# A fused two-block kernel: another order for the recurrence that runs between block products

## The reference, cut to what matters

```python
proj = h @ w_in[l]                       # g_q, g_f, g_i, g_z are 8 heads x 128 columns each
q = silu(q_raw); logf = log(lb + (1 - lb) * sigmoid(fr)); k = (1 - lb) * sigmoid(-fr)
def step(S, xs):
    qn, kn, vn, ln = xs
    b = cumsum(ln, axis=2)
    b_last = b[:, :, -1]
    inter = einsum('bhcd,bhde->bhce', qn * exp(b), S)
    diff = b[:, :, :, None, :] - b[:, :, None, :, :]
    decay = exp(where(tril, diff, -inf))
    A = einsum('bhtd,bhtsd,bhsd->bhts', qn, decay, kn)
    intra = einsum('bhts,bhse->bhte', A, vn)
    k_dec = kn * exp(b_last[:, :, None, :] - b)
    S_new = exp(b_last)[..., None] * S + einsum('bhsd,bhse->bhde', k_dec, vn)
    return S_new, inter + intra
```

## Time and profile before

| | |
|---|---|
| three runs, median (lowest to highest) | 1989.35 us (1988.53 to 1993.09) |
| profiled execution: its own time | 1990.67 us |
| profiled execution: span of the trace | 1988.9 us |
| PE, DVE, ACT, POOL busy | 94%, 74%, 47%, 15% |
| seven steps of pairs, 1258.02 to 1756.38 us | 498.36 us |
| in them PE, DVE, ACT busy | 383.80, 308.88, 238.16 us |

### The profile page before, as it was taken

How to read it: one execution, slowest core, us unless ns; L and a number is a source line. 1 busy time by engine, 2 the same in 40 slices (tenths; PEclk the granted TensorE clock), 3 DMA queues, 4 the chain that set the end, 5 groups by cost and what they waited for, 6 DMA issues and landing times.

```text
span 1988.9 us, 30107 instructions
## 1 busy us (share of the span) xinstructions
PE 1860.4 (94%) x11014; PEld 1649.0 (83%) x11014; DVE 1470.0 (74%) x2190; ACT 926.6 (47%) x1406; POOL 289.9 (15%) x283
## 2 busy tenths in 40 slices
PE   9999999999999999999999999868778777789999
PEld 8888888888888878878899999867777776778999
DVE  6666688888888876688787877756566566558986
ACT  6543433333333633245565666635445435446433
POOL 3500000000000024420011111031132122111021
PEclk9999999999999999999999999979978888899999
DMA  6244244444444356744477777444453444462452
GB/s 266 106 171 168 82 167 172 171 169 169 169 170 174 121 202 231 248 166 137 117 201 193 184 198 193 117 102 101 106 118 95 105 114 107 108 210 85 139 179 86
DMA packets 80505, 304.07 MB, mean 153 GB/s; under 512 B 8584, under 2 KB 14216, under 8 KB 67728
## 3 DMA queue, kind: packets, MB, share of 16 engines
q1 hardware_dynamic: 66640, 256.49, 37.3%
q0 software_dynamic: 13312, 43.00, 12.2%
q10 hardware_dynamic: 448, 3.17, 0.4%
HBM read 288.44 MB, written 14.18 MB: 152 GB/s over the span
## 4 chain that ended last, share of the span: by engine, by line
PE 75%; DVE 11%; ACT 7%; issue 6%; DMA 1%; POOL 0%; DVEq 0%; POOLq 0%; ACTq 0%; SPq 0%; another core or an unknown queue 0%
PE ps_p L918 13%; PE ps_p L920 13%; PE ps_p L919 13%; PE ps_p L1322 4%; PE ps_p L1321 4%; PE ps_p L1323 4%; ACT w_hi L1917 2%; DVE w_lo L2917 1%; PE ps_o L1083 1%; PE ps_t L1571 1%; PE ps_t L1572 1%; PE ps_t L1570 1%; PE ps_t L1067 1%; PE ps_s L1571 1%; PE ps_s L1570 1%
## 5 line engine op out<-in xcount | busy, mean ns | idle before, releaser
L918 PE MATMUL ps_p<-act_hi,w_hi 128*128 128x512 f32 x1232 | 490.0, 398 | 0.3 <-DVE w_lo L2371 0.3
L920 PE MATMUL ps_p<-act_hi,w_lo 128*128 128x512 f32 x1232 | 480.7, 390 | 0.0
L919 PE MATMUL ps_p<-act_lo,w_hi 128*128 128x512 f32 x1232 | 479.8, 389 | 0.0
L1594 ACT ACTIVATE w_hi<-raw 128x2048 fp32r<-128x2048 f32 x88 | 168.5, 1915 | 268.2 <-PE ps_p L920 251.4
L920 PEld LDWEIGHTS ps_p<-act_hi,w_lo 128*128 128x128 f32 x1232 | 231.2, 188 | 49.8
L918 PEld LDWEIGHTS ps_p<-act_hi,w_hi 128*128 128x128 f32 x1232 | 231.5, 188 | 46.5 <-issue 1.2
L919 PEld LDWEIGHTS ps_p<-act_lo,w_hi 128*128 128x128 f32 x1232 | 231.7, 188 | 44.8 <-issue 0.7
L1322 PE MATMUL ps_p<-y_lows,w_hi 128*128 128x256 f32 x832 | 242.5, 291 | 0.0
L2366 DVE TENSOR_TENSOR w_lo<-raw,w_hi 128x2048 fp32r<-128x2048 f32 x86 | 197.4, 2295 | 48.6 <-ACT w_hi L1594 41.8
L2917 DVE TENSOR_TENSOR w_lo<-raw,w_hi 128x1024 fp32r<-128x1024 f32 x118 | 146.3, 1241 | 76.1 <-ACT w_hi L1917 74.3
L1322 PEld LDWEIGHTS ps_p<-y_lows,w_hi 128*128 128x128 f32 x832 | 165.9, 199 | 0.2
(11 more groups left out here) (563 smaller groups left out, 4427.1 us busy)
## 6 DMA issues: line engine op xcount, KB each, us to landing
raw<-wt_dram SPq DMA_DIRECT2D x94, 1024.0 KB, 4.8
raw<-wt_dram SPq DMA_DIRECT2D x124, 512.0 KB, 4.3
mkv<-ada_dram SPq DMA_DIRECT2D x96, 512.0 KB, 4.4
raw<-wt_dram POOLq DMA_DIRECT2D x40, 512.0 KB, 7.6
mkv<-wt_dram POOLq DMA_DIRECT2D x38, 512.0 KB, 6.7
mkv<-wt_dram SPq DMA_DIRECT2D x12, 512.0 KB, 5.0
qkv<-xT_dram SPq DMA_DIRECT2D x16, 256.0 KB, 2.8
spill_dram<-Y SPq DMA_DIRECT2D x16, 256.0 KB, 2.5
```

Source lines behind the costliest of these rows:

```text
L918: mm(o, wh, hi[:, k, 0:n], start=at == 0, stop=False)
L919: mm(o, wh, lo[:, k, 0:n], start=False, stop=False)
L920: last = mm(o, wl, hi[:, k, 0:n], start=False, stop=at == KT - 1)
L1594: fn(w_hi[:, s, :], raw[:, s, :], ACT.Copy).then_inc(w_hi_done, 1)
```

## The change

It moves calls among the four engines' `hg_pairs`. On PE, level 7 moves from F0 to F1, levels 0 to 6 move one product later or more, the keys from S2 to S3, turned pairs and states into F2's end. On ACT, `pair_high` of S1, S2 and S4 and `first_form(second)` stand earlier, `out_rows` later, the exponential of level 7 goes to the end of the step it belongs to, and F2's high part to the next step. On DVE `pair_low` of S3 and S4 stand earlier, `output` later. POOL's last level and decayed query move to the end of their own step. `first_form` of a second pair goes to a place of its own (`HG_CORNER`, in `mkv`). Level 0's difference on DVE (L3202) is dropped: ACT takes the exponential in three instructions of 128 columns with a bias operand.

```diff
@@ -556,2 +556,3 @@
         PAIR_OUT = ((qkv2[:, 0, :], qkv2[:, 1, :]), (qkv2[:, 2, :], wk[:, 3, :]))
+        HG_CORNER = mkv[:, 0, 1, :]
         HG_OUT = ((hd[:, 0, :], hq), (hvT[:, :], wk[:, 3, :]))
@@ -578,2 +579,6 @@
+        def first_kept(q):
+
+            return HG_CORNER if q >= ATT_PAIRS and q % 2 else pair_out(q)[1][:, EARLY_TOKENS]
+
         def pair_out(q):
...
                 else:
-                    pe.wait_ge(bank_read.sem, bank_read.at("pair", q, (2, 1, 3)[n - 4]))
+                    pe.wait_ge(bank_read.sem, bank_read.at("pair", q, ((1, 2, 3) if h >= 0 and v else (2, 1, 3))[n - 4]))
@@ -1459,7 +1464,6 @@
                 if i:
-                    pair_product(first, 0, {1: level(i - 1, NLEV - 1)})
+                    pair_product(first, 0, {4: level(i - 1, NLEV - 2)})
                     turn_hg(i - 1)()
-                    pair_product(first, 1)
-                    turn_pairs(i - 1)()
-                    pair_product(first, 2, {3: chunk_states(i - 1)})
+                    pair_product(first, 1, {5: level(i - 1, NLEV - 1)})
+                    pair_product(first, 2, {4: turn_pairs(i - 1), 6: chunk_states(i - 1)})
                     pair_product(first, 3)
@@ -1468,4 +1472,4 @@
                     pair_product(first, 5)
-                    pair_product(first, 6)
-                    pair_product(second, 0, {1: out_sum(i - 1)})
+                    pair_product(first, 6, {2: out_sum(i - 1)})
+                    pair_product(second, 0)
                 else:
@@ -1485,7 +1489,7 @@
                 pair_product(second, 1)
-                pair_product(second, 2, {3: turn_keys(i), 6: level(i, 0)})
-                pair_product(second, 3, {4: level(i, 1)})
-                pair_product(second, 4, {1: level(i, 2), 6: level(i, 3)})
-                pair_product(second, 5, {4: level(i, 4)})
-                pair_product(second, 6, {1: level(i, 5), 6: level(i, 6)})
+                pair_product(second, 2)
+                pair_product(second, 3, {6: turn_keys(i)})
+                pair_product(second, 4, {1: level(i, 0), 5: level(i, 1)})
+                pair_product(second, 5, {2: level(i, 2), 6: level(i, 3)})
+                pair_product(second, 6, {3: level(i, 4), 7: level(i, 5)})
@@ -1506,3 +1510,3 @@
                 pe.wait_ge(bank_read.sem, bank_read.at("pair", NPAIR - 1, 4))
-                hooks = {0: level(i - 1, NLEV - 1), 3: turn_hg(i - 1), 5: turn_pairs(i - 1), 6: chunk_states(i - 1)}
+                hooks = {0: level(i - 1, NLEV - 2), 4: level(i - 1, NLEV - 1), 1: turn_hg(i - 1), 6: turn_pairs(i - 1), 7: chunk_states(i - 1)}
                 for at, k in enumerate(range(HALF_K, KT)):
@@ -2027,8 +2031,9 @@
                 act.wait_ge(product_done.sem, product_done.at("pair", q, 1))
-                if h > 0:
-                    busy = (heads_done if q % 2 else query_decayed)
-                    act.wait_ge(busy.sem, busy.at("hg", h - 1, 1))
+                if h >= 0 and q % 2:
+                    act.wait_ge(bank_read.sem, bank_read.at("pair", q - 2, 5))
+                elif h > 0:
+                    act.wait_ge(query_decayed.sem, query_decayed.at("hg", h - 1, 1))
                 elif q % 2:
                     act.wait_ge(s_att, 16 * (q // 2 + NPLAIN))
-                fn(pair_out(q)[1][:, EARLY_TOKENS], pair_first(q), ACT.Copy).then_inc(corner_copied.sem, 1)
+                fn(first_kept(q), pair_first(q), ACT.Copy).then_inc(corner_copied.sem, 1)
@@ -2125,3 +2130,8 @@
                 if n == 0:
-                    fn(hkd[:, 0:S - HCHUNK], d[:, 0:S - HCHUNK], ACT.Exp, scale=-1.0).then_inc(level_exps.sem, 1)
+                    for t in range(NCH - 1):
+                        c = slice(t * HCHUNK, (t + 1) * HCHUNK)
+                        last = fn(hkd[:, c], hbk[:, c], ACT.Exp, scale=-1.0, bias=hb[:, c.stop - 1:c.stop])
+                        if t < NCH - 2:
+                            o.step(last)
+                    last.then_inc(level_exps.sem, 1)
                     return
@@ -2130,4 +2140,2 @@
                     fn(d[:, 0:S // 2], d[:, 0:S // 2], ACT.Exp).then_inc(level_exps.sem, 1)
-                    act.wait_ge(pair_sum_in.sem, pair_sum_in.at("hg", i, 1))
-                    fn(sq3_hi[:, 0:S // 2], d[:, 0:S // 2], ACT.Copy).then_inc(pair_sum_high.sem, 1)
                     return
@@ -2138,2 +2146,6 @@
+            def pair_highs(i):
+                act.wait_ge(pair_sum_in.sem, pair_sum_in.at("hg", i, 1))
+                fn(sq3_hi[:, 0:S // 2], hd[:, (NLEV - 1) % 2, 0:S // 2], ACT.Copy).then_inc(pair_sum_high.sem, 1)
+
             def hg_softplus(i, k, dst, src):
@@ -2200,3 +2212,4 @@
                     hg_softplus(i - 1, 3, wk[:, 2, :], wk[:, 3, :])
-                    level_exp(i - 1, NLEV - 1)
+                    pair_highs(i - 1)
+                    pair_high(first, 2)
                     first_form(first)
@@ -2225,21 +2238,22 @@
                 pair_high(second, 0)
-                hg_softplus(i, 1, wk[:, 1, :], hd[:, 0, :])
                 pair_high(second, 1)
+                hg_softplus(i, 1, wk[:, 1, :], hd[:, 0, :])
+                pair_high(second, 2)
                 forgets(i)
-                if i:
-                    out_rows(i - 1)
+                first_form(second)
                 hg_softplus(i, 2, wk[:, 2, :], hq)
-                pair_high(second, 2)
-                hg_sigmoid(i, 2)
                 decay_row(i)
                 pair_high(second, 3)
-                for n in range(3):
-                    level_exp(i, n)
-                first_form(second)
+                hg_sigmoid(i, 2)
+                level_exp(i, 0)
+                level_exp(i, 1)
+                pair_high(second, 4)
+                level_exp(i, 2)
                 diag(i)
+                if i:
+                    out_rows(i - 1)
                 keys_turned(i)
-                pair_high(second, 4)
                 level_exp(i, 3)
-                level_exp(i, 4)
                 pair_high(second, 5)
+                level_exp(i, 4)
                 first_corner(second)
@@ -2250,4 +2264,4 @@
                     level_exp(i, 6)
+                    level_exp(i, 7)
                     pair_high(second + 1, 1)
-                    pair_high(second + 1, 2)
                 else:
@@ -2255,2 +2269,3 @@
                     level_exp(i, 6)
+                    level_exp(i, 7)
                     turn_tile(1)
...
                 if n == 0:
+                    if h >= 0 and q % 2:
+                        if h:
+                            dve.wait_ge(heads_done.sem, heads_done.at("hg", h - 1, 1))
+                        else:
+                            dve.wait_ge(s_att, 16 * NATT)
                     dve.wait_ge(corner_copied.sem, corner_copied.at("pair", q, 1))
-                    ins = tt(x1[:, LATE_TOKENS], PAIR_SECOND, x1[:, EARLY_TOKENS], ALU.add)
+                    ins = tt(x1[:, LATE_TOKENS], PAIR_SECOND, first_kept(q), ALU.add)
...
@@ -3199,10 +3221,5 @@
                 if n == 0:
-                    n3 = NCH - 1
-                    r = blocks(hb[:, :], HCHUNK)[:, 0:n3, HCHUNK - 1:HCHUNK].broadcast_to([P, n3, HCHUNK])
-                    tt(blocks(d, HCHUNK)[:, 0:n3], blocks(hbk, HCHUNK)[:, 0:n3], r, ALU.subtract).then_inc(
-                        level_diff.sem, 1)
+                    dve.sem_inc(level_diff.sem, 1)
                     return
-                if n == 2:
-                    dve.wait_ge(level_exps.sem, level_exps.at("hg", i, 1))
-                elif n > 2:
+                if n > 2:
                     dve.wait_ge(level_in.sem, level_in.at("hg", i, n - 2))
@@ -3322,5 +3339,6 @@
                     masked(i - 1, NLEV - 3)
-                    pair_lows(i - 1)
                     masked(i - 1, NLEV - 2)
                     z_log(i - 1)
+                    pair_lows(i - 1)
+                    pair_low(first, 2)
                     pair_low(first, 3)
@@ -3332,11 +3350,11 @@
                     odd_pairs(i - 1)
+                    states(i - 1)
                     read_pair(first, 1)
                     pair_low(first, 5)
-                    states(i - 1)
                     pair_low(first, 6)
-                    read_pair(first, 2)
                     pair_sum(second)
+                    read_pair(first, 2)
+                    square_lo("hg", i - 1, 0, sq3_hi[:, :], sq3_lo[:, :])
                     pair_low(second, 0)
                     read_pair(first, 3)
-                    square_lo("hg", i - 1, 0, sq3_hi[:, :], sq3_lo[:, :])
                 else:
@@ -3369,18 +3387,19 @@
                 pair_low(second, 2)
-                query_log(i, hq)
                 decays(i)
-                for n in range(3):
-                    diff(i, n)
+                diff(i, 0)
+                query_log(i, hq)
+                diff(i, 1)
+                pair_low(second, 3)
                 queries(i, hq)
                 dve.sem_inc(query_ready.sem, 1)
+                diff(i, 2)
```

(23 more changed lines are left out.)

38 lines of the change are left out of this document (19 added, 19 removed).

## The result

The changed kernel takes 1911.11 us (1908.98 to 1912.65, 4 runs) where the kernel before takes 1991.22 beside it (1988.53 to 1993.61, 4 runs): ratio 0.9597 with the interval 0.9579 to 0.9615, so 80 us or 4.0% faster. The forecast was 1892 in a range of 1866 to 1930.

The account below looks back on a forecast made before the run. Bound: a chain crossing engines at fixed places of the order. Savings of 74.1 (steps 1 to 5), 13.1 (step 6) and 10.8 (step 0), less 1 (tail), are 97.0 us off 1990.67: 1892 as median, range 1866 to 1930.

Parts of the forecast that it names:

- PE's own work: PE's busy time per step at full clock, products plus small groups, levels and keys: 47.1 us, the floor.
- The old waits: PE's waits at level 7 (7.3 us) and ahead of S2 (4.85 us) go; 0.6 remains at level 7.
- A at S6: New PE wait ahead of S6, behind exponential 5, high part, low part and a read: 3.2 us a step.
- B at the keys: New PE wait at the keys, for ps_x, which ACT's later out_rows still holds: 1.0 us a step.
- C at S5: New PE wait ahead of S5, with ten DVE instructions instead of four between S4's and S5's low parts: 2.5 us.
- The four small ones: Short new PE waits: F0' 0.15, turned values 0.1, F2's low part 0.4, turned pairs 0.2 us a step.
- The three exponentials: Level 0's split exponential on ACT: 0.9 to 1.2 us for 0.505 and one DVE difference, hidden from the keys.
- The clock: One fall of PE's clock a step, around the waits at S5 and S6: 2.0 us, bounds 0 and 5.4.
- The tail: After the last step: level 7's 5 us go, but act_hi's reload goes out some 3 us later; loss of 1.
- The first: Rival: clock stays low through the second pair and F0', 7 us a step more than counted; 1941 us, chance 0.12.
- The second: Rival: gains at level 7 and S2 come back in full at S6 and S5; 1985 us, chance 0.06.
- The third: Rival: POOL's fourth sum lands late for F5; 1946 us, or about 2000; chance 0.06, of which 0.03 slower.

Follow-up runs that it names:

- s6_high_ahead: Changed kernel with S6's high part on ACT put ahead of the first corner and the exponential of level 5; 1891.33 us, ratio 0.9498.
- waits_filled: Changed kernel with useless matmuls on PE, 22 ahead of S5 and 26 ahead of S6, to keep it busy through the waits; 1900.05 us.
- s5_low_ahead: Changed kernel with S5's low part on DVE put ahead of difference 4 and level 1's mask; 1892.58 us, ratio 0.951.
- old_order_filled: Kernel before the change with useless matmuls filling PE's waits, 36 ahead of S2 (24 in step 0) and 56 at level 7; 1986.83 us.
- reload_early: Changed kernel with the tail's reload of act_hi issued on POOL ahead of level 4's product of the last step; 1901.68 us, ratio 0.955.
- reload_alone: Changed kernel with act_hi's reload issued early, Y's reload held until act_lo has landed, and the head's weights loaded ahead of it; 1894.59 us.
- s2_high_only: Kernel before the change with only S2's high part on ACT moved ahead of the forgets; 1976.84 us, ratio 0.9926.

## Why the prediction was right

**The result** lies 19 us above the forecast and inside the range. By steps it is 2.0 us a step (59.2 for 57.2, 14 us over seven) and 4.3 us in the tail. Not every sign came: three steps have a granted clock of 0.91 or 0.92, where I had named 0.93 or more, and four take 59.6 to 61.3 us, where I had named 55 to 59.

**PE's own work: right, but the edges of the waits were left out.** I worked out 47.1 us a step; the full-clock step of `s6_high_ahead` has 48.64 busy, and step 2 of `waits_filled` 54.18 less its 48 fillers of 0.12, 48.4. That is 1.5 us a step, 10.8 in all, more than half the miss. The start times in that step of `s6_high_ahead` tell where it lies. The 336 matmuls of products at 0.12 are 40.1 us, as I had them. The small groups are 6.25 us, and behind twelve of them the first spacing is 0.20 in place of 0.12, 1.0 more: 7.2 for my 6.9. Five of the twelve stand in the stretch that I had measured whole; the other seven, the keys and six levels, I had priced at 0.36 without it. The other 1.3 us stand at the step's six waits: the last matmul ahead of one counts as busy for 0.28 where the next would have come after 0.12, which is 0.16 each, and behind four of them the first spacing is 0.20 or more. So each wait costs some 0.2 us beyond its idle time, and that term was missing.

**The old waits: right.** Level 7 fell from 48.7 to 0.8 us, S2 to nothing. I had 0.6 a step at level 7, and it shows only where PE comes early enough: at clock 1.00, with the waits filled, it is up to 0.9.

**New waits: right.** A at S6 3.2, measured 3.22. B at the keys 1.0, measured 1.00 in step 2 and up to 1.3. C at S5 2.5, measured 2.88. The four small ones (0.85 together) are not in the list of the changed kernel. All idle time of PE is 54.1 / 7 = 7.7 us a step for the 8.15 I summed. `s6_high_ahead` and `s5_low_ahead` show the causes, exponential 5 and DVE's pieces between the low parts: without them the waits are 1.4 and mostly 1.45.

**The three exponentials: right.** The 128-column instruction with a bias takes 0.388 us on average; three take 0.98 from the first's start to the last's end, within 0.9 to 1.2, and the keys wait once for them, 0.4 us. By the Trainium skill, ScalarE: Activation LUTs, Rules for kernel authors, the prediction's estimate was 0.41 for each; the trace agrees to 0.02 us.

**The clock: the size right, in part by luck.** Busy time is 51.47 where full clock would have 48.64, 2.8 us a step. Some of it is given back by shorter waits, and `waits_filled` puts the net at 1.6 to 2.3; I had 2.0. But I had counted one fall a step for the two waits together, and the trace has two in four of the seven steps. Measured, a step is 48.6 + 2.8 + 7.7 = 59.2 where I had 47.1 + 2.0 + 8.1 = 57.2. What failed is the view that I took into `old_order_filled`, that such a term can be added to any order: there a third to a half of the lower level went and brought 3 us, where I expected 25 to 35.

**The tail: mis-sized.** I counted 1 us and it was 5.3. I saw the late issue, but priced it by the delay alone; the landing also grew, from 14.4 to 16.7 us. `reload_early` and `reload_alone` show what I missed: issued well ahead of `Y`'s reload, `act_hi` lands in 5.9, and with `Y`'s reload held back `act_lo` falls from 16.0 to 7.3.

**The rivals.** The first, the clock low through the whole second pair and F0', did not come, though the clock fell more often than I had it: in step 2 matmuls are 0.12 apart again 3 us behind S5's wait, low from 1429.94 and at 0.12 once more from 1433.3. The second, a shift of waits and no gain, did not come for the change, but S2's move alone comes near it (`s2_high_only`: 14 us won, where seven waits of 4.85 us are 34). The third, the fourth sum late, did not come: POOL's sums land in 6.3 us for 5.5, and nobody waits for them.
